# Row maxima taken two blocks at a time, with the two matmuls of a pair in different halves of TensorE's rows

## The reference, cut to what matters

```python
def gqa_dense(q, k, v, sink=None):
    scale = HEAD_DIM ** -0.5
    def attend(qb):
        s = jnp.einsum('bqhgd,bkhd->bhgqk', qb, k, preferred_element_type=F32) * scale
        ...
            p = jax.nn.softmax(s, axis=-1)
        return jnp.einsum('bhgqk,bkhd->bqhgd', p.astype(v.dtype), v)
    return sweep_queries(attend, (q,))
```

## Time and profile before

| what | value |
|---|---|
| median of three runs | 3619.41 us (3611.78 to 3621.05) |
| the profiled execution: its own time, its span | 3618.99 us, 3617.2 us |
| granted TensorE clock, mean | 0.989 |
| busy: PE, DVE, ACT, POOL | 3456.4, 2400.3, 2155.9, 1272.3 us |
| attention of MLA, GQA, SWA, MLA | 401 to 926, 1337 to 1805, 2199 to 2525, 2984 to 3494 us |

### The profile page before, as it was taken

How to read it: one execution, slowest core, us unless ns; L and a number is a source line. 1 busy time by engine, 2 the same in 40 slices (tenths; PEclk the granted TensorE clock), 3 DMA queues, 4 the chain that set the end, 5 groups by cost and what they waited for, 6 DMA issues and landing times. The chain is left out here.

```text
span 3617.2 us, 82216 instructions
## 1 busy us (share of the span) xinstructions
PE 3456.4 (96%) x33644; PEld 2060.7 (57%) x33644; DVE 2400.3 (66%) x3920; ACT 2155.9 (60%) x2859; POOL 1272.3 (35%) x1315
## 2 busy tenths in 40 slices
PE   6999999999999989999999998999999999999998
PEld 3554566666555556666645556666455446666654
DVE  6426688888466639999846517887553458888854
ACT  5424687887434438888823226887343338888861
POOL 0000255555230016666612003666120005555542
PEclk9999999999999999999999999999999999999999
DMA  6127523332112443333111335442112482222211
GB/s 256 52 86 218 158 69 78 82 82 65 68 36 59 130 122 74 82 75 74 43 73 52 96 115 131 109 113 69 69 46 69 134 224 56 56 56 60 53 50 59
DMA packets 373333, 325.50 MB, mean 90 GB/s; under 512 B 246272, under 2 KB 294080, under 8 KB 371424
## 3 DMA queue, kind: packets, MB, share of 16 engines
q1 hardware_dynamic: 372960, 320.24, 32.5%
HBM read 228.94 MB, written 91.23 MB: 89 GB/s over the span
## 5 line engine op out<-in xcount | busy, mean ns | idle before, releaser
L2421 POOL TENSOR_TENSOR p_lo<-p_f,p_hi 128x512 f16<-128x512 f32 (+2 forms) x768 | 836.3, 1089 | 725.2 <-DVE p_lo L2357 402.2
L2233 PE MATMUL bank<-q_slots,k_slots 96*128 96x512 f16 (+7 forms) x3968 | 1047.0, 365 | 30.3 <-PEq L1436 16.2
L798 PE MATMUL bank<-H_hilo,w_hilo 128*128 128x512 f16 (+1 forms) x5760 | 1044.7, 344 | 13.9 <-DVE w_hilo L1048 9.3
L2052 DVE TENSOR_REDUCE max_parts<-bank 128x1 f32<-128x512 f32 (+2 forms) x1536 | 959.9, 646 | 111.0 <-PE bank L1996 97.1
L2309 ACT ACTIVATE p_f<-bank 128x1024 f32<-128x1024 f32 (+2 forms) x768 | 743.5, 968 | 260.5 <-PE bank L2233 246.4
L798 PEld LDWEIGHTS bank<-H_hilo,w_hilo 128*128 128x128 f16 x5760 | 563.4, 98 | 495.0 <-DVE w_hilo L1048 10.3
L2316 ACT ACTIVATE p_hi<-bank 128x1024 f16<-128x1024 f32 (+2 forms) x768 | 743.6, 968 | 0.0
L2357 DVE TENSOR_TENSOR p_lo<-p_f,p_hi 128x512 f16<-128x512 f32 (+2 forms) x768 | 578.6, 753 | 155.4 <-ACT p_hi L2316 149.2
L1996 PE MATMUL bank<-k_slots,q_slots 96*128 96x512 f16 (+4 forms) x1536 | 561.8, 368 | 23.4 <-DVE max_parts L2052 13.1
L2233 PEld LDWEIGHTS bank<-q_slots,k_slots 96*128 96x128 f16 (+2 forms) x3968 | 345.0, 98 | 294.1 <-issue 49.4
L1012 ACT ACTIVATE z_ring<-bank 128x512 f32<-128x512 f32 (+1 forms) x192 | 87.5, 528 | 429.4 <-PE bank L798 416.1
(11 more groups left out here) (205 smaller groups left out, 4004.0 us busy)
## 6 DMA issues: line engine op xcount, KB each, us to landing
ada_w<-in_w_ada SPq DMA_DIRECT2D x48, 768.0 KB, 6.4
gate<-z_ring SPq DMA_DIRECT2D x32, 640.0 KB, 3.3
gate_rows<-gate SPq DMA_DIRECT2D x32, 640.0 KB, 4.0
q_slots<-q_mla SPq DMA_DIRECT2D x64, 240.0 KB, 3.3
k_mla<-H_hilo SPq DMA_DIRECT2D x64, 224.0 KB, 3.2
k_slots<-k_mla SPq DMA_DIRECT2D x64, 224.0 KB, 4.6
cq_hilo<-v_scratch SPq DMA_DIRECT2D x64, 224.0 KB, 4.2
v_lo_hi_one<-v_scratch SPq DMA_DIRECT2D x64, 224.0 KB, 4.2
```

The costliest lines, as they stand in the source:

```text
L798: ins = pe.matmul(dst, lhs(a, k), rhs(b, k), start=(k == 0 and n == 0), stop=(k == nk - 1 and n == 2))
L2052: found = dve.tensor_reduce(mx[:, o, t, c:c + 1], mb[:, 0:nk], AX.X, ALU.max)
L2233: scored = pe.matmul(dst, lhs, rhs, start=(m == 0), stop=(m == len(ops) - 1), skip_group_check=swa)
L2421: pool.tensor_tensor(pl[:, g % 4, cols // 2:cols], p32[:, g % 3, cols // 2:cols], ph[:, g % 4, cols // 2:cols], ALU.subtract).then_inc(s_p ...
```

## The change

1. A "max" entry is now a pair of blocks: two matmuls into the two banks of `bank[2]` (`PAIR`), and one reduction over both. In MLA and GQA it gives two columns of `max_parts` ([P, 2, 512] in); in SWA, where both blocks belong to the same queries, one column over both.
2. In GQA and SWA the matmuls of a pair contract over 64 rows each: the first over rows 0 to 63 of part 0 of Q (q high), the second over rows 64 to 127 of part 1 (q high too), both against k high. q low has no part in the maximum any more. In the built program these are matmuls with array tiles of [64, 128] at row 0 and at row 64, 352 of each; all other tiles are as before.
3. For that, part 1 has q high and k low in rows 64 to 127, the maximum and the constant in row 0, and zeros in rows 1 to 63, which GpSimd writes at the start of `values`. The matmul of 65 rows in the scores is one of 128 rows.
4. `own` and `ahead` place one pair in each step; in SWA no pair in some. Pairs always use `PAIR`, every other entry `ONE` (`bank[3][:, 1]`), each waiting for the last of its kind. All "max" and "turn" entries of a step stand after its first score block, "ada" after the second, "out" after P x V. VectorE takes the pair before `p_lo`, the others after.

```diff
-        mx = sb("max_parts", [P, 3, 4, 3], F32)
+        mx = sb("max_parts", [P, 3, 12], F32)
...
+        PAIR, ONE = bank[2], bank[3][:, 1]
...
-                pool.memset(K[row:row + 1, :, 1, :], MAX_UNIT).then_inc(s_row.h, 1)
+                pool.memset(Q[0:HD, :, 1, :], 0.0).then_inc(s_row.h, 1)
+                pool.memset(K[0:HD, :, 1, :], 0.0).then_inc(s_row.h, 1)
+                pool.wait_ge(s_row.h, s_row.base + 2)
+                pool.memset(K[0:1, :, 1, :], MAX_UNIT).then_inc(s_row.h, 1)
...
                 self.wait_gates(act)
+                act.wait_ge(s_row.h, s_row.base + 1)
...
-        for dst, src in ((Q[:, h % 3, 0], q), (Q[0:HD, h % 3, 1], q[0:HD])):
+        for dst, src in ((Q[:, h % 3, 0], q), (Q[HD:P, h % 3, 1], q[0:HD])):
...
+            return [("max", u, n // 2, blocks[n:n + 2]) for n in range(0, len(blocks), 2)]
...
-            own = [b_[6:9], b_[9:11] + c_[:1], b_[11:] + c_[1:], [turn(1)], [turn(2)]] + [[]] * 8
-            ahead = [[]] * 4 + [a_[:2], a_[2:4], a_[4:6], a_[6:8], a_[8:10], a_[10:], b_[:3], mod + b_[3:4],
-                                [turn(0)] + b_[4:6]]
+            own = [b_[1:2], b_[2:3], b_[3:4], b_[4:5], b_[5:6], [turn(1)] + c_, [turn(2)]] + [[]] * 6
+            ahead = [[]] * 6 + [a_[0:1], a_[1:2], a_[2:3], a_[3:4], a_[4:5] + mod, a_[5:6], [turn(0)] + b_[0:1]]
...
-                    (K[0:HD + 1, ks, 1, kt_cols], Q[0:HD + 1, qs, 1, q_cols])]
+                    (K[:, ks, 1, kt_cols], Q[:, qs, 1, q_cols])]
...
-                kk = MLA_QK if mla else P
-                ins = pe.matmul(mb[:, 0:nk], Q[0:kk, q_slot(hd, hb), 0, q0:q0 + P],
-                                K[0:kk, k_slot(hd, hb), 0, k0:k0 + nk],
-                                start=True, stop=True, skip_group_check=bool(masks))
+                for half, (t, k0, nk, masks) in enumerate(blocks):
+                    q0 = units[u][0] + t * P
+                    part = slice(0, MLA_QK) if mla else slice(half * HD, half * HD + HD)
+                    ins = pe.matmul(mb[:, half, 0:nk], Q[part, q_slot(hd, hb), 0 if mla else half, q0:q0 + P],
+                                    K[part, k_slot(hd, hb), 0, k0:k0 + nk],
+                                    start=True, stop=True, skip_group_check=bool(masks))
...
-            found = dve.tensor_reduce(mx[:, o, t, c:c + 1], mb[:, 0:nk], AX.X, ALU.max)
+            if swa and u < 2:
+                found = dve.tensor_reduce(mx[:, o, n2:n2 + 1], mb[:].rearrange("p b n -> p (b n)")[:, 0:PAST + nk],
+                                          AX.X, ALU.max)
+            else:
+                found = dve.tensor_reduce(mx[:, o, 2 * n2:2 * n2 + 2], mb[:, :, 0:nk], AX.X, ALU.max)
```

More of the change, by code:

```diff
@@ L1747, in maxima_of @@
             q0, nq = units[u]
-            found = []
-            for t in range(nq // P):
-                if u == 2:
-                    found.append(("max", u, t, 0, PAST + LAT, CTX, []))
-                elif not swa:
-                    found += [("max", u, t, c, c * 512, 512, []) for c in range(3)]
-                else:
+            tiles = range(nq // P)
+            if u == 2:
+                blocks = [(t, PAST + LAT, CTX, []) for t in tiles]
+            elif not swa:
+                blocks = [(t, c * 512, 512, []) for t in tiles for c in range(3)]
+            else:
+                blocks = []
+                for t in tiles:
                     i = q0 // P + t
@@ L2248, in body @@
                         if p < P2:
-                            for k in todo[2:]:
+                            for k in of_kind(b, todo, "out"):
                                 emit_entry(pe, i, b, k)
```

70 lines of the change are left out of this document (35 added, 35 removed).

## The result

Four runs of the changed kernel gave 3647.84 to 3651.37 us, median 3649.16; the kernel before, on the same chip, 3618.6 (3611.78 to 3621.05, 4 runs). The ratio is 1.0088, with a 95% interval of 1.0071 to 1.0106: slower by about 30 us. That is outside the predicted range, on the slow side, where a gain of 21 us had been forecast. The granted clock is the same (0.990 against 0.989 over the span), so the difference is not one of clock.

The account below looks back on a forecast made before the run. TensorE alone was taken to bound MLA; GQA held 30 us of waiting among three close engines. Terms MLA -5, GQA -14, SWA 0, stages before -3 and +1 sum to -21: from 3619.0 to 3598 us, range 3568 to 3640.

Parts of the forecast that it names:

- Two halves, two switches: Row-half pairs in GQA and SWA: 0.20 us of switches against 0.215 gained, so pairs of 512 columns gain nothing.
- cheaper switches: Rival: row halves drain less than column strips, giving back 42 us of work in GQA, 25 in SWA; 3570; chance 0.14.
- the halves don't run at once: Rival: a pair's halves run one after the other, 0.20 us more per pair; about 3655 us; chance 0.10.
- The reduction: VectorE's one reduction of 1024 takes 1.13 us against 1.20 for two, counted only in the waits.
- The stages before: `values` before GQA and SWA: waits removed, memsets of about 3 us added; GQA -3 us, SWA +1.
- The added work: SWA's pairs with shorter halves lose to the switches: 0.54 us per head, +8.7 us.
- one pair per step, one pair of banks: Attention's new table: VectorE frees the pair's banks in time but for bursts; GQA's waiting about 15 us instead of 30.
- MLA: Both MLA attentions: slack everywhere, a few waits removed, 4 us in the first layer and 1 in the last: -5 us.
- GQA: GQA attention: waiting -15 us, short pairs +1.5, about -14 us.
- SWA: SWA attention: 8.7 us of work added, turns wait 13 us, 9 us less of idle and hidden time: 0.
- the waits come back: Rival: one pair of banks allows no running ahead, 15 to 40 us more in GQA and SWA; 3610 to 3635; chance 0.22.
- the single pair of banks in MLA: Rival: a pair's reduction over 1.8 us makes each MLA step lose the excess; 3640 and more; chance 0.06.

Follow-up runs that it names:

- Kernel 5: The changed kernel with both MLA attentions put back to three banks, single maxima and the old table of steps; 3625.8 us, ratio 1.0025.
- Kernel 7: The changed kernel with unit 0's output of the second head in step 10 instead of 11 in MLA and GQA (ada in step 9); 3640.6 us.
- Kernel 8: The changed kernel with the edits of kernel 3 and Kernel 7 together; 3629.1 us, ratio 1.0034.
- Kernel 12: The kernel before, GQA alone changed: two single maxima per step, three banks, turns after second score block, both maxima reduced before `p_lo`; 3605.0 us, GQA 456.1.
- kernel 9: kernel 6 with GQA's pairs contracting over all 128 rows, and SWA given late-turn pairs over all rows; 3616.3 us, GQA 463.6.
- kernel 6: The kernel before with the change in GQA alone, there with kernel 3's late turns and the output in step 10; 3599.6 us, GQA 456.4.
- kernel 3: The changed kernel with turns of units 0 and 1 after the second score block and the last small reduction written to SBUF; 3628.4 us.
- kernel 2: The changed kernel with unit 0's output of the second head in step 9 instead of 11 in MLA and GQA; 3748.7 us.

## Why the prediction was wrong

**Right.** *Two halves, two switches.* 3 ns between the halves, 0.10 in and 0.10 out against 0.215: the column strips of the trace before priced the row halves exactly. The rule of the Trainium skill (TensorEngine Tiling, Key Properties) that a change of mode drains the engine agrees with this trace, which has its price in both directions. The rivals "cheaper switches" and "the halves don't run at once" are out. *The reduction*, 1.13 us: 1.14. *The stages before* the attentions: three memsets of 3.1 to 3.3 us and 1.6 us of TensorE's waiting are as forecast. In the pair of traces these stages changed by -2.3 us (GQA) and -0.2 (SWA), where -3 and +1 were said, but such a stage varies by several us between kernels that share its code. Averaged over all kernels here, with the new stage against without it, GQA's is 2.7 us shorter and SWA's 3.4 longer. So GQA's term was right, and SWA's was near only by luck. In SWA the removed waits were sized rightly too: by starts all waits that are neither switches nor turns fall from some 39 to 17 us, about the 22 that were implied. The added work was 5 to 7 us, depending on what is taken for the usual turn, not 8.7. One slip in a rival changes nothing: 144 pairs in SWA at 0.2 us are 29 us, not 25.

**Wrong: the step "one pair per step, one pair of banks", in its parts on the turn.** It followed the pair's banks only. It priced the turn by neg_max alone, and never asked what else stands in `ONE`, the other bank, which turn, ada and output now share; the diff said so in one line.

- *MLA*, -5 predicted, +20.8 measured. The step "TensorE is back after 2.45 + 0.65 = 3.10, ... neg_max at 3.0. Slack remains everywhere" failed twice. It took a full step for the short step 12, whose first block is 0.33 long and not 0.65: TensorE arrives some 0.3 early, and in the first heads, with no output in the way, 0.33 is lost. And in the second heads the turn stands behind the output in one bank: 0.99 lost. By starts 9.7 and 9.8 us, where nothing had been priced. Kernel 5 shows that all of the 20.8 us comes with MLA's new scheme. Kernel 7 shows that the bank's part of the turn's wait is about half, and that in MLA 2 most of this half was lost again elsewhere. Kernel 8 shows the limit of this account: with the turns' waits all but gone, only 4.9 and 0.9 us came back. So the scheme is the cause by experiment, the turns are where its cost first stood, and why the rest stays is open. That MLA had to be the safe place, "with TensorE busy for 99% of the stage", was the wrong way round: a stage with no idle time pays for each new wait in full.
- *GQA*, -14 predicted, -2.6 measured. Here the prediction did see the short step. It gave the turn in step 5 a wait of 0.2 us, the one in step 12 a wait of 0.4 in every other head, and none in the heads with an output in step 11: "(there the output's transposes give time)". Measured by starts: 0.35, 0.57, and 1.22 in just those heads, since the output occupies the bank. Together that is 18.8 us before turns where 6.4 had been summed. The waits that the change was to remove went for the larger part.
- *SWA*, 0 predicted, +9.5 measured: 27.9 us before turns, 13 expected. There it is largely the ada rows, copied out by VectorE, that hold the bank (10.0 us in 7 waits).

Together the turns cost 66 us by starts, 10 in the kernel before; 19 had been priced. None of the rivals was this: "the waits come back" had GQA's banks and stayed at 3635, "the single pair of banks in MLA" had the right stage and the wrong bank.

**Also wrong: where GQA's gain lies.** The sum gave the gain to fewer bank waits through the pair. Kernel 12 has it all with singles and three banks. Of the change's own parts in GQA, the halves are worth 7 us in a design of one reduction for both (kernel 9 against 6), and pair and halves together nothing against singles well placed (kernel 6 against 12).

**Left open.** What keeps MLA 7 to 8 us above before in kernel 8 is known by place, and was not tried apart. The most direct trial of the shared bank, one of its own for the turns or three banks beside late turns in MLA, was not run. In kernel 3 SWA gave back 4.6 of its 9.5 us though 18 us of turn waits went; the rest is not explained either. Whether kernel 12's order would help MLA and SWA too was not run.

## What to carry to other kernels

When a change merges or splits buffers, list for every buffer all kinds of entries that will share it, and follow each from its write to its release in the shortest step, not the full one: the entry that nobody costed was the one that blocked. Don't take the sum of a wait row for what its removal gives: here most of the removed waits stood again at another place. A stage whose bottleneck engine is 99% busy has no room for new waits. And before crediting a new instruction form with a gain, run the new schedule with the old instructions.

## What the hardware did that was not expected

- Two matmuls in different halves of the rows start 3 ns apart and share a record of 0.39 us, and the switch costs 95 ns in and 103 ns out by the timeline's starts, the same 0.10 each way as for column strips of 32. For pairs of 512 columns that cancels the gain in TensorE's time (0.016 us left), but the second result is there 0.11 us sooner.
- One reduction of 1024 columns, 1220 ns long, takes 1.14 us from start to start, against 1.20 for two of 512.
- A wait of about 2.5 us in every pair of heads (kernel 2) went with a granted clock of 0.95 in MLA 1 instead of 0.99, and of 0.972 over the span instead of 0.990.
- Weight loads can show a long total wait at no cost: 61.3 us of waiting for `max_parts` in the GQA of kernel 6, the fastest, against 21.6 before.
